# Root-mean-square norms of the head tiles done in groups: mean squares of many tiles gathered in one bank, one root and one reciprocal for a group, spread back by selector products

## The reference

```python
def rms_norm(x, g):
    y = xf * lax.rsqrt(jnp.mean(xf * xf, axis=-1, keepdims=True) + EPS)
    return y * g
# per layer
xn = rms_norm(x, norm1_g)
z = xn @ w_in
p_a, q_b, k_b, v_b, h_c, b_c, c_c, q_d, k_d, v_d = split_cols(z, SPLITS)
# q_b, k_b: rms_norm over the 64 channels of a head; q_d, k_d: over 32
y_a = pool_mixer(p_a, w_pool)                     # causal means of 2, 4, 8, 16 tokens, per-group linear
y_b = swa_sink_attention(q_b, k_b, v_b, ...)      # window 128, 4 heads
y_c = short_conv_mixer(h_c, b_c, c_c, conv_w)
y_d = diff_attention(q_d, k_d, v_d, ...)          # two softmax maps per head, 4 heads
# head_norm: rms_norm over the 64 channels of each head
y = concatenate([head_norm(y_a), head_norm(y_b), head_norm(y_c), head_norm(y_d) * (1 - lam_init)])
x = x + y @ w_out
x = x + peer_ffn(rms_norm(x, norm2_g), ...)       # 8 heads x 16 experts per token, rows of peer_u and peer_v
```

## Time and profile before

| | |
|---|---|
| median of 3 runs | 3017.1 us (3016.74 to 3018.5) |
| the profiled execution's own time | 3016.79 us |
| its span | 3015.0 us |
| busy PE, DVE, ACT, POOL | 70%, 71%, 38%, 39% |
| bytes moved | 1170.89 MB, of which 1073.81 MB by the gathers |
| reciprocals of L816 | 60 |

### The profile page before, as it was taken

One profiled execution on the slowest core, in us unless ns is written; L12 is line 12 of the kernel. 1 busy time (PEld: TensorE's weight loads), 2 busy tenths in 40 slices (PEclk: granted clock), 3 DMA queues, 4 the chain that ended last, 5 costly groups with the idle time before them and its releaser, 6 DMA issues.

```text
span 3015.0 us, 37523 instructions
## 1 busy us (share of the span) xinstructions
PE 2096.9 (70%) x12704; PEld 1044.6 (35%) x12704; DVE 2147.9 (71%) x5267; ACT 1130.8 (38%) x3444; POOL 1184.8 (39%) x1028
## 2 busy tenths in 40 slices
PE   7867788667877777576776777567777556555655
PEld 6654454224443433133342344224343111111111
DVE  4545688987657878877666877986766777776665
ACT  3422445653224445533223545652322222222222
POOL 0023343344444344343344344344434444444443
PEclk9789899788988888788898889778899766777687
DMA  4169999999999999999999999999999999999998
GB/s 161 63 245 419 383 416 420 384 355 419 419 419 420 419 420 416 362 358 419 420 420 420 417 402 420 403 374 393 420 419 421 421 419 419 420 414 420 415 412 345
DMA packets 173840, 1170.89 MB, mean 388 GB/s; under 512 B 19280, under 2 KB 19408, under 8 KB 42576
## 3 DMA queue, kind: packets, MB, share of 16 engines
q0 software_dynamic: 147456, 1073.81, 86.6%
q1 hardware_dynamic: 26192, 94.68, 8.2%
HBM read 1166.32 MB, written 2.10 MB: 388 GB/s over the span
## 4 chain that ended last, share of the span: by engine, by line
DMA 39%; DVE 24%; PE 21%; ACT 9%; issue 6%; POOL 1%; DVEq 0%; SPq 0%; POOLq 0%; ACTq 0%
DMA gather<-experts,idx 39%; DVE gather L1039 12%; PE ysum L548 12%; PE bank L406 5%; DVE sd L816 3%; ACT diag L755 2%; PE bank L507 2%; ACT amp L747 2%; ACT L597 1%; POOL gather L364 1%; ACT gel L740 1%; DVE x L1016 1%; DVE shared L843 1%; ACT sd L597 1%; PE bank L453 1%
## 5 line engine op out<-in xcount | busy, mean ns | idle before, releaser
L364 POOL DMA_INDIRECT gather<-experts,idx x1024 | 1184.6, 1157 | 1808.5 <-PE ysum L548 1461.6
L548 PE MATMUL ysum<-gather,diag 64*64 64x512 f32 x8192 | 1264.3, 770 | 781.0 <-ACT diag L755 735.2
L1039 DVE CUSTOM_DVE_ANT_0 gather<-gather,xc 128x1024 f32<-128x1024 f32 x1024 | 1223.6, 1223 | 559.9 <-DMA gather<-experts,idx 557.0
L548 PEld LDWEIGHTS ysum<-gather,diag 64*64 64x64 f32 x8192 | 366.3, 172 | 1581.6 <-ACT diag L755 945.1
L740 ACT ACTIVATE gel<-hdot 128x4 f32<-128x4 f32 x255 | 52.4, 205 | 1627.9 <-DVE hdot L1039 1627.9
L406 PE MATMUL bank<-xnT,w 128*128 128x256 f32 x1984 | 470.1, 392 | 12.4 <-DVE xnT L805 12.4
L406 PEld LDWEIGHTS bank<-xnT,w 128*128 128x128 f32 x1984 | 378.3, 195 | 110.6 <-issue 45.5
L755 ACT ACTIVATE diag<-cc,amp 128x64 f32<-128x64 f32 x1020 | 268.7, 333 | 2.9 <-PE ysum L548 2.8
L747 ACT ACTIVATE amp<-gel,gate 128x1 f32<-128x1 f32 x1020 | 216.8, 283 | 8.3
L816 DVE RECIPROCAL sd<-sd 128x256 f32<-128x256 f32 x60 | 105.1, 1751 | 119.1 <-ACT sd L597 118.9
L740 ACT ACT_TABLE_LOAD x124 | 159.1, 1283 | 2.2
(11 more groups left out here) (116 smaller groups left out, 1497.0 us busy)
## 6 DMA issues: line engine op xcount, KB each, us to landing
w<-weights SPq DMA_DIRECT2D x168, 512.0 KB, 7.9
gather<-experts,idx POOLq DMA_INDIRECT x1024, 14.0
y_out<-x SPq DMA_DIRECT2D x4, 512.0 KB, 8.4
x<-x_in SPq DMA_DIRECT2D x2, 512.0 KB, 5.1
g2b<-g_rows SPq DMA_DIRECT2D x2, 512.0 KB
x<-x_in SPq DMA_DIRECT2D x1, 1024.0 KB, 11.9
cc<-consts_in SPq DMA_DIRECT2D x1, 635.5 KB, 5.8
late<-late_in SPq DMA_DIRECT2D x2, 256.0 KB, 9.9
```

The lines of the kernel that those rows point to most:

```text
L364: pool.indirect_dma_start(gather[:, n % SLOTS, :], None, uv_d[m // 2], bass.IndirectOffsetOnAxis(ap=idx[:, g % 2, k:k + 1], axis=0)).then_ ...
L548: mm = nc.tensor.matmul(ysum[outs, q * 512:(q + 1) * 512], diag[toks, n % NDIAG, :], gather[toks, n % SLOTS, DM + hf * 512:DM + (hf + 1) * ...
L1039: e = V.tensor_tensor_reduce(out=gather[:, n % SLOTS, 0:DM], in0=gather[:, n % SLOTS, 0:DM], in1=xc[:, :], scale=1.0, scalar=0.0, op0=ALU. ...
```

## The change

The 15 norms of a block become three groups. A group's squares are kept apart: those of the z tiles in `sq_z`, a free part of `shared`, those of the output tiles in `sq_y`, which is `xnT`. PE multiplies the squares of tile n by a selector of 1/64 or 1/32 that puts the mean squares of its two or four heads into rows of their own of one bank, and adds the tiles of the group up in that bank (`sum_squares`). ACT takes one root of 128 x 256, DVE one reciprocal. Then PE multiplies 32 rows of the reciprocal by a 32 x 128 selector of ones, which gives in every partition of a tile the value of its head (`spread`, two tiles to a bank), and DVE multiplies tile, gain and that bank.

The groups are: the seven z tiles (sum in slice z7, root there, reciprocal in slice 8, spread and products in slice 9); output tiles 0 to 5 (squares in steps 9 to 11, sum and root in step 12, reciprocal in step 13, spread and products in step 14); output tiles 6 and 7 (squares in steps 15 and 16, sum, root and reciprocal in one more slice, spread and products in another). The constants grow from 1271 to 1841 columns of 128 float32. The weights in `work` change with it: the z slices from 8 to 6, 6, 6, 6, 6, 6, 6, 8, 6, 12, the last norm from one slice of 10 to two of 6.

```diff
+YSQ_AT = {9: (0, 1), 10: (2, 3), 11: (4, 5), 15: (6,), 16: (7,)}
+YSUM_AT = 12
-    return ([9, 6, 6] + [8] * (NORMED + NV) + [6] + [11] * 8 + [12 if half else 10] * (ITEMS - 7)
-            + [10] * (8 - ITEMS + POOL_AT) + [8] * 8 + [9, 6, 6] + [8, 8, 2] * HEADS + [3] * 4)
+    return ([9, 6, 6] + [6] * NORMED + [8, 6, 12] + [6] + [11] * 8 + [12 if half else 10] * (ITEMS - 7)
+            + [6] * 2 + [8] * 8 + [9, 6, 6] + [8, 8, 2] * HEADS + [3] * 4)
-        sq = sb("sq", 2, HALF)
+        sq_z = shared[:, 10 * HALF:(10 + NORMED) * HALF].rearrange("p (i t) -> p i t", t=HALF)
+        sq_y = xnT
+            def sum_squares(name, tiles):
+                ps = start(name)
+                for n in tiles:
+                    pe.wait_ge(s_sq, 15 * m + n + 1)
+                    row, groups = norm_rows(n)
+                    first = CC_S64 + 30 - row if groups == 2 else CC_S32 + 28 - row
+                    mm = nc.tensor.matmul(ps[:, 0:HALF], cc[:, first:first + P],
+                                          sq_z[:, n, :] if n < NORMED else sq_y[:, n - NORMED, :],
+                                          start=n == tiles[0], stop=n == tiles[-1])
+                mm.then_inc(s_ready, 1)
+            def spread(name, group, tiles):
+                ps = start(name)
+                pe.wait_ge(s_root, group)
+                for i, n in enumerate(tiles):
+                    rows, first = spread_at(n)
+                    mm = nc.tensor.matmul(ps[:, i * HALF:(i + 1) * HALF], cc[rows, first:first + P],
+                                          sd[rows, (group - 1) % 2, :], start=True, stop=True)
+                mm.then_inc(s_ready, 1)
...
-                if 0 < i <= NORMED:
-                    ps = start(("n", i - 1))
-                    pe.wait_ge(s_sq, 15 * m + i)
-                    nc.tensor.matmul(ps[:, 0:HALF], ones64 if i - 1 <= ZKB else ones32, sq[:, (15 * m + i - 1) % 2, :],
-                                     start=True, stop=True).then_inc(s_ready, 1)
+                if i == NORMED:
+                    sum_squares(("zs", 0), range(NORMED))
+                if i == NORMED + NV - 1:
+                    for j in range(4):
+                        spread(("zb", j), 3 * m + 1, range(2 * j, min(2 * j + 2, NORMED)))
...
-                if a > POOL_AT:
-                    sum_squares(a - POOL_AT - 1)
+                if a == YSUM_AT:
+                    sum_squares(("ys", 0), range(NORMED, NORMED + YA))
+                if a == YSUM_AT + 2:
+                    for j in range(3):
+                        spread(("yb", j), 3 * m + 2, range(NORMED + 2 * j, NORMED + 2 * j + 2))
+            sum_squares(("ys", 1), range(NORMED + YA, NORMED + 8))
+            yield
+            spread(("yb", 3), 3 * m + 3, range(NORMED + YA, NORMED + 8))
+            yield
...
-            def normalise(n, tile, gain):
-                nn = 15 * m + n
-                done(dve, m, ("n", n) if n < NORMED else ("y", n - NORMED))
-                chain(dve, V.reciprocal(sd[:, nn % 2, :], sd[:, nn % 2, :]))
-                V.scalar_tensor_tensor(tile, tile, gain, sd[:, nn % 2, :], ALU.mult, ALU.mult).then_inc(s_nrm, 1)
+            def reciprocal_root(name, group):
+                done(dve, m, name)
+                V.reciprocal(sd[:, group % 2, :], sd[:, group % 2, :]).then_inc(s_root, 1)
+            def normalise(name, tiles):
+                ready(dve, m, name)
+                for n, (tile, gain) in enumerate(tiles):
+                    e = V.scalar_tensor_tensor(tile, tile, gain, bank_of(m, name)[:, n * HALF:(n + 1) * HALF],
+                                               ALU.mult, ALU.mult)
+                e.then_inc(s_done["dve"], 1)
```

More of the change, by code:

```diff
@@ L581, in x_rms, with square, root @@
                     yield
-            def square(n, src):
-                nn = 15 * m + n
[L586 to L593, removed]
-                ready(act, m, name)
[L595 to L598, removed]
+            def square(n, dst, src):
+                nc.scalar.activation(dst, src, ACT.Square).then_inc(s_sq, 1)
+            def root(name, group):
+                ready(act, m, name)
+                if group >= 2:
+                    pm, pg = divmod(group - 2, 3)
+                    ready(act, pm, (("zb", 3), ("yb", 2), ("yb", 3))[pg])
+                nc.scalar.activation(sd[:, group % 2, :], bank_of(m, name)[:, 0:HALF], ACT.Sqrt, bias=eps)\
+                    .then_inc(s_done["act"], 1)
             def empty(name, out, in_):
@@ L618, in mixer_act @@
                     done(act, m, ("z", i))
-                    square(i, z_home(i, half))
+                    square(i, sq_z[:, i, :], z_home(i, half))
                 else:
@@ L679, in mixer_act @@
                         empty(("pool", j), yT[:, j, :], bank_of(m, ("pool", j))[:, 0:HALF])
[L680 to L683, removed]
+                for n in YSQ_AT.get(a, ()):
+                    square_y(n)
+                if a == YSUM_AT:
+                    root(("ys", 0), 3 * m + 1)
                 if half and a + ahead < ITEMS:
@@ L687, in mixer_act @@
                 yield
[L688 to L692, removed]
+            root(("ys", 1), 3 * m + 2)
+            yield
+            yield
             for i in range(8):
@@ L827, in mixer_dve @@
             for i in range(NORMED + NV):
-                if 0 < i <= NORMED:
-                    normalise(i - 1, z_home(i - 1, half), zcol(layer, SP_QKG + i - 1))
+                if i == NORMED + 1:
+                    reciprocal_root(("zs", 0), 3 * m)
+                if i == NORMED + NV - 1:
+                    for j in range(4):
+                        normalise_z(j)
                 yield
@@ L938, in mixer_dve @@
                     attn_weights(a + 1)
-                if a > POOL_AT:
-                    normalise_y(a - POOL_AT - 1)
+                if a == YSUM_AT + 1:
+                    reciprocal_root(("ys", 0), 3 * m + 1)
+                if a == YSUM_AT + 2:
+                    for j in range(3):
+                        normalise_y(j)
                 yield
-            for n in range(ITEMS - POOL_AT, 8):
-                normalise_y(n)
-                yield
+            reciprocal_root(("ys", 1), 3 * m + 2)
+            yield
+            normalise_y(3)
+            yield
             for i in range(8):
@@ L1138, in layout_consts @@
     c[:, CC_ID:CC_ID + P] = np.eye(P)
-    c[:, CC_O64:CC_O64 + P] = q // 64 == np.arange(P)[None] // 64
-    c[:, CC_O32:CC_O32 + P] = q // 32 == np.arange(P)[None] // 32
+    c[:, CC_S64:CC_S32] = np.where((np.arange(P + 30)[None] - 30) % GROUPS == q // 64, 1 / 64, 0)
+    c[:, CC_S32:CC_SPREAD] = np.where((np.arange(P + 28)[None] - 28) % GROUPS == q // 32, 1 / 32, 0)
+    for n in range(NORMED + 8):
+        row, groups = norm_rows(n)
+        for g in range(groups):
+            rows, first = spread_at(n)
+            c[rows.start + row + g, first + g * P // groups:first + (g + 1) * P // groups] = 1.0
     dist = q + 128 - np.arange(256)[None]
```

63 lines of the change are left out of this document (35 added, 28 removed).

## The result

The changed kernel takes 2987.96 us (median of 4 runs, 2987.07 to 2992.77), the kernel before beside it 3016.92 us: ratio 0.9909, 95% interval 0.9897 to 0.9921, so 29 us faster. The forecast was 2974, within 2957 to 3003: the direction and the place of the gain were right, its size was 43 and is 29.

The account below looks back on a forecast made before the run. Transfers at 419 GB/s set the pace, except where DVE's list bound the norm stretches, and in block 0. From 3016.8 us: constants +0.8, block 0 +3.7 and -5, first projections +1, norm stretches -43, giving 2974; range 2957 to 3003.

Parts of the forecast that it names:

- The bound and the place: Behind the first gather, only stretches below 419 GB/s can gain; DVE's list is the chain in three norm stretches: 43 us.
- Reciprocals and waits for roots: Per norm stretch of mixers 1 to 3: six fewer reciprocals save 10.5 us; fewer root waits save 9.8, 13.6, 5.3.
- the quarter I kept: Norm stretches: two of eight root waits remain, so three quarters of 13.1, 18.1 and 7.1 us go.
- the estimate of 55 us: Norm stretches: with the skill's drain, each of 18 removed waits holds 1.4 us more, moving the gain to 55.
- New waits in the norm stretches: DVE waits for PE's spread in step 14 and the last slice: 2 us each, 4 per stretch; bounds nothing and 7.1.
- rival 3: First projections: PE holds slice 9's spreads until DVE's reciprocal, freeing no slots; 18 us per stretch gives 3027; chance 0.06.
- First projections: Mixers 1 to 3: fewer reciprocals gain nothing under transfers; two projections per gap lose 1 us in all, bounds 0 and 10.
- Block 0: Before the first gather: seven spreads ahead of the scores cost 3.7 us; norms up to the output projection save 5.
- the constants: Start of block 0: 0.29 MB more ahead of ACT's first square costs 0.8 us, upper bound 2.6.
- Sum: Whole kernel: 3016.8 + 0.8 + 3.7 - 5 + 1 - 43 = 2974.3 us.
- the main case: Whole kernel: the terms hold as summed, 2974 us, own range 2964 to 2988; chance 0.60.

Follow-up runs that it names:

- the two runs above: Kernel before without its 32 output-tile reciprocals: 2972.65 us; changed kernel with six unawaited reciprocals put back in each mixer: 3003.05 us.
- the split runs: Changed kernel with no second slice in attention gaps (S, a0 to a16, first extra slice): 2974.99 us; second extra slice alone too: 2970.76 us.
- The first split run: Changed kernel, but no second slice put into a gap with S, a0 to a16 or the first extra slice: 2974.99 us, ratio 0.9871.
- The version with the selectors loaded late: Changed kernel with z norms one by one, S, a0 to a16 and both extra slices alone, selectors loaded behind the weights: 2968.34 us, ratio 0.9847.

## Why the prediction was right, and where it was off

**The bound and the place.** Right. Behind the first gather only stretches below 419 GB/s gave anything; the norm stretches gave 40 us against a forecast of 43. The run without reciprocals confirms that DVE's list was the chain.

**Reciprocals and waits for roots.** Right in kind; how the 40 us split between the two is not settled, since the shares in the two runs above do not add up. Of 38.3 us of waits for a root 4.3 stayed, less than the quarter I kept. The root's table load still costs what the trace of before said, and no drain stands behind it. The chain of the changed kernel near the last root of mixer 3:

```profile
2003.44 1.28 ACT L635
2004.74 0.48 ACT sd L635
2005.25 1.76 DVE sd L851
```

The root begins 0.02 us behind the load. The 1380 ns of drain that the Trainium skill gives ("ScalarE: Activation LUTs", "What ACT_TABLE_LOAD costs") do not show here, and the estimate of 55 us that hung on them did not come about.

**New waits in the norm stretches.** Mis-sized on the wrong engine. I priced the spread as DVE waiting for PE, 2 us each, and DVE waited just 2.2 us once in each of mixers 2 and 3. The costly side was PE waiting for DVE's reciprocal, 12.4 us in mixer 2 and 9.4 in mixer 3 with `ysum` behind it. I had that mechanism as rival 3, but looked for it at slice 9, and did not list which dependent slices the numbers put into one gap in each mixer. It left 6.9 and 6.5 us, where I took 2 and 1 off; the split runs got most of it back.

**First projections, "I take 1 us of new loss in all; bounds 0 and 10".** This is the step that failed most: 5.7 + 4.1 + 0.6 = 10.4 us. The reason I gave, two projections in a gap, was not it; the pair S and a0 was. The first split run keeps all projections in their gaps and parts that pair, and loses nothing there. In mixer 1 the new numbers made the pair; in mixer 3 it was there before, and what it cost rose.

**Block 0.** First scores at 62.06 in place of 56.31, of which the constants made 1.8 (landed after 7.6 us in place of 5.8; I took 0.8, with 2.6 as the bound) and the spreads 3.9 (3.7 forecast). The 1.8 is one pair of executions: over all profiles the 1841 columns landed after 6.4 to 7.6 us, and the 1271 of the kernels with the list of before after 5.7 to 6.3, so my 0.8 is not refuted. From the scores to the end of the output projection 5.6 us were gained (5 forecast). The granted clock rose there too, from 0.57 to 0.86 in 101 to 134, for which I had counted nothing. The run with the reciprocals put back tells the two apart: with a clock of 0.84 it takes 109.1 us from the scores to that end, before it was 108.4, in the changed kernel 102.7. So the gain goes with the reciprocals, and not with the clock. Then the second input norm and the first queries:

```profile
171.90 9.06 PE L428 MATMUL bank<-xnT,w 128*128 128x256 f32 x32 [0.78 <-DVE xnT L841]
...
192.18 1.08 POOL L386 DMA_INDIRECT gather<-experts,idx  x1 [191.73 <-DVE idx L1047]
```

These 32 passes took 7.17 us before, at a granted clock of 1.00 (2.4 GHz); here it was 0.76 in 171 to 181, so partly at 1.2 GHz, with the same list. So block 0 came out 1.9 us later where I had 0.5 earlier. That is one pair of executions. In its second profile the changed kernel starts its gathers at 189.10, and the kernel before with the new numbers of `work`, whose list in block 0 is that of before, at 188.06: 1.0 later. The clock step has no term in the forecast, and the two profiles do not settle how much of it belongs to the change.

**Sum.** Forecast -43 + 1 - 0.5 = -42.5. Measured: -40 in the norm stretches, +10.4 of new losses, -2 of small ones elsewhere that are gone, +1.9 in block 0, +0.7 for the constants' bytes: -29. The stated range held; of the main case's own, 2964 to 2988, the 2987.96 lies at the edge. The new losses were ten times what I took, and above their own bound of 10.

## What to carry to other kernels

Where two engines run interleaved lists that stand on opposite sides of a shared piece of work, a pair of slices that depend on each other should not fall into one gap: such a pair cost 3 to 7 us here where DVE was late, and nothing in two places where PE waited 0.85 and 2.7 us. Taking them apart was worth about 20 us, two thirds of what the change itself gave. After any edit of slice costs, list which slices share a gap in each round, and look there for the wait of the engine that frees the buffers. And read a gain only where the bound engine is the one relieved: 18 of the 48 reciprocals removed stood under the transfers and were worth nothing, while their replacement cost 4 us in the part where nothing was hidden.

## What was not expected of the hardware

PE's clock moved the start of the gathers by 2 us with an unchanged list: 32 matmul passes of 128x256 took 7.17 us at a granted clock of 1.00 and 9.06 at 0.76. It goes either way even in one kernel. The version with the selectors loaded late was profiled twice:

```profile
165.05 9.60 PE L439 MATMUL bank<-xnT,w 128*128 128x256 f32 x32 [0.88 <-DVE xnT L869]
```

```profile
166.99 7.17 PE L439 MATMUL bank<-xnT,w 128*128 128x256 f32 x32 [1.30 <-DVE xnT L869]
```

The granted clock was 0.72 in the first (165 to 174) and 1.00 in the second (167 to 174). What decides was not settled, and a difference of 2 to 3 us in block 0 between two single profiles cannot be put down to the kernels. Nor does the granted clock of a row tell all: the first 32 projection passes of block 0 took 9.39 us in the profile of before and 7.17 in that of the same list with new numbers of `work`, and both rows (16 to 25) show 1.00.
